# Twelve more u tiles turned during the merge stage, with the loads reordered, out units begun early and the sort spread evenly

## The reference

```
a = att_out @ w_att_branch ; b = ml_out @ w_ml_branch
x = x + (sigmoid(ga) * a + sigmoid(gb) * b) @ w_out
q = norm(x) @ wq ; s = q . sub_keys ; top 16 per half, then top 16 of the sums
out = sum over picks of g * gelu(u[pick] . xn) * v[pick]
```

## Time and profile before

| | |
|---|---|
| median of 3 runs | 1986.28 us (1985.18 to 1992.99) |
| profiled execution | 1996.68 us, span 1994.9 us, mean granted PE clock 0.979 |
| busy shares of the span | PE 96%, VectorE 69%, ACT 44%, POOL 39% |
| project | 0 to 480.5 us |
| merge | 480.5 to 611.5 us |
| queries | 611.5 to 680 us |
| search, steps 0 to 127 | 680 to 1396.2 us |
| experts and finish | 1396.2 to 1994.9 us |

### The profile page before, as it was taken

How to read it: one execution, slowest core, us unless ns; L and a number is a source line. 1 busy time by engine, 2 the same in 40 slices (tenths; PEclk the granted TensorE clock), 3 DMA queues, 4 the chain that set the end, 5 groups by cost and what they waited for, 6 DMA issues and landing times. The chain is left out here.

```text
span 1994.9 us, 32364 instructions
## 1 busy us (share of the span) xinstructions
PE 1907.0 (96%) x11569; PEld 1810.7 (91%) x11569; DVE 1368.2 (69%) x2630; ACT 885.1 (44%) x1929; POOL 775.0 (39%) x639
## 2 busy tenths in 40 slices
PE   6999989998798999999999999999999999999998
PEld 6978868887797999999999999999999999999997
DVE  3133555665514399899999877776678777778775
ACT  4031022224314245678787888782333333333333
POOL 4433323332223346665566666571122222222210
PEclk9989989999998999999999999999999999999999
DMA  7612159887552145799999999999799999999982
GB/s 173 115 50 64 43 164 234 263 271 223 195 107 74 47 152 174 243 272 287 283 296 291 285 311 325 311 314 311 247 345 330 352 342 332 352 334 342 352 300 94
DMA packets 325341, 478.79 MB, mean 240 GB/s; under 512 B 37533, under 2 KB 250013, under 8 KB 321853
## 3 DMA queue, kind: packets, MB, share of 16 engines
q1 hardware_dynamic: 287740, 341.63, 55.7%
q0 software_dynamic: 36864, 134.23, 20.9%
q10 hardware_dynamic: 576, 0.85, 0.1%
HBM read 391.52 MB, written 83.96 MB: 238 GB/s over the span
## 5 line engine op out<-in xcount | busy, mean ns | idle before, releaser
L1468 PE MATMUL ps<-x_high,split_high 128*128 128x416 f32 x1024 | 370.9, 362 | 18.2 <-DVE split_low L1455 16.9
L1468 PE MATMUL ps<-x_high,split_low 128*128 128x416 f32 x1024 | 362.1, 354 | 0.0
L2111 PE MATMUL ps<-hid_high,split_high 128*128 128x416 f32 x1024 | 358.9, 350 | 1.7 <-PEq L1689 1.7
L1468 PE MATMUL ps<-x_low,split_high 128*128 128x416 f32 x1024 | 360.3, 352 | 0.0
L2111 PE MATMUL ps<-hid_low,split_high 128*128 128x416 f32 x1024 | 358.8, 350 | 0.0
L2111 PE MATMUL ps<-hid_high,split_low 128*128 128x416 f32 x1024 | 358.7, 350 | 0.0
L2054 ACT CAST split_high<-area 128x1024 fp32r<-128x1024 f32 x127 | 133.3, 1049 | 383.5 <-PE ps L2111 382.5
L1337 POOL DMA_INDIRECT gathered_rows<-in_peer_v_dram,gathered_index x128 | 133.9, 1046 | 420.0 <-DVE gathered_acc L1374 343.2
L2082 DVE TENSOR_TENSOR split_low<-area,split_high 128x1024 fp32r<-128x1024 f32 x127 | 155.6, 1225 | 134.2 <-ACT split_high L2054 134.2
L1337 POOL DMA_INDIRECT gathered_rows<-in_peer_u_dram,gathered_index x128 | 157.1, 1227 | 215.2 <-DVE gathered_rows L1352 189.3
L1468 PEld LDWEIGHTS ps<-x_high,split_high 128*128 128x128 f32 x1024 | 193.4, 189 | 25.7 <-DVE split_low L1455 21.5
(11 more groups left out here) (299 smaller groups left out, 3844.8 us busy)
## 6 DMA issues: line engine op xcount, KB each, us to landing
area<-in_peer_v_dram SPq DMA_DIRECT2D x128, 512.0 KB, 5.5
u_nat<-in_peer_u_dram SPq DMA_DIRECT2D x392, 128.0 KB, 5.8
routing<-dense SPq DMA_DIRECT2D x26, 1024.0 KB, 6.5
area<-hidden SPq DMA_DIRECT2D x128, 208.0 KB, 7.3
hidden<-gelu_out SPq DMA_DIRECT2D x124, 208.0 KB, 4.7
w_raw<-in_w_in_dram SPq DMA_DIRECT2D x44, 512.0 KB, 5.8
mv_nat<-in_peer_u_dram SPq DMA_DIRECT2D x120, 128.0 KB, 3.6
u_nat<-turned_u SPq DMA_DIRECT2D x30, 512.0 KB, 3.7
```

Source lines behind the costliest of these rows:

```text
L1468: ins = self.nc.tensor.matmul(self.k.ps[:, b, 0:N], w[:, b, kk, :], x[:, kk, 0:N], start=(kk == 0 and p == 0), stop=(kk == KD - 1 and p == 2))
L2111: ins = nc.tensor.matmul(ps[:, kk, 0:N], v[:, b, kk * P:(kk + 1) * P], h[:, b, :], start=(n == 0 and p == 0), stop=(n == P - 1 and p == 2))
```

## The change

Three things are changed. Tiles 30 to 41 are turned ahead too, in the merge, by the same code, which becomes a class `Ahead`: six turns follow the branch units 5, 7, ... 15 on VectorE, six follow the adds of out units 1, 3, ... 11. SP's list in the merge is put in another order: gate blocks 0 and 1 without a wait, chunk 2 before gate blocks 2 and 3, x not before c = 3; tile loads and stores come in from c = 3 on, before the query weights where the list has them so, and the last six tiles' stores and loads after all query weights. The out units take all eight banks, and the first four of them do the first six of their eight blocks of rows as soon as 12 low halves are there and the gated products of unit 13 are done. In the search the plan's credit is 1.5 from step 28 on where it was 1.8 from step 30, so the fourth and fifth frame tiles are sorted at steps 54 and 84. Buffers: the squares of the norm go into the gates' tile, which makes room for the turned tiles.

```
-AHEAD = 30
+EARLIER, MERGED = 30, 12
+AHEAD = EARLIER + MERGED
...
+    BEGUN, FIRST_PART = 4, 6
...
+    BESIDE_BRANCH = MERGED // 2
+    def turned_by(u):
+        return [EARLIER + (u - 5) // 2] if u >= 5 and u % 2 else []
+    def turned_in(u):
+        return [EARLIER + BESIDE_BRANCH + u // 2] if u % 2 and u // 2 < MERGED - BESIDE_BRANCH else []
+    def slot(j):
+        return (j + 2) % RING
...
+            def turned_ones(first, count):
+                for n in range(first, first + count):
+                    ahead.store(sp, n)
+                    if n + 2 < AHEAD:
+                        ahead.load(sp, n + 2)
...
                 if c == 1:
+                    for j in range(2):
+                        load_gates(j)
+                if c == 2:
                     sp.wait_ge(mo_used, 4)
-                    for j in range(RING):
+                    for j in range(2, RING):
                         load_gates(j)
+                if c == 3:
                     sp.dma_start(x[:, 0:4, :], x_prompt[0].rearrange("(t p) d -> p t d", p=P)).then_inc(x_loaded, 16)
...
+                if c == 3:
+                    for n in range(EARLIER, EARLIER + 2):
+                        ahead.load(sp, n)
+                if 4 <= c < 7:
+                    turned_ones(EARLIER + 2 * (c - 4), 2)
                 if c == 6:
...
             load_queries(1)
+            turned_ones(EARLIER + BESIDE_BRANCH, MERGED - BESIDE_BRANCH)
             sp.wait_ge(k.loaded, 16 * QUARTERS)
+            for h in range(2):
+                sp.wait_ge(k.u_stored[h], 16 * AHEAD)
...
-            pe.wait_ge(merged_low_done, 2 * KD - 1)
...
-                if u >= 4:
-                    pe.wait_ge(out_added, u - 3)
-                for kk in range(KD):
+                if u >= 8:
+                    pe.wait_ge(out_added, u - 7)
+                for kk in range(lo, hi):
...
+            pe.wait_ge(merged_low_done, 2 * FIRST_PART)
+            pe.wait_ge(a_used, 2 * (2 * KD - 2))
+            for u in range(BEGUN):
+                out(u, 0, FIRST_PART)
+            pe.wait_ge(merged_low_done, 2 * KD)
+            for u in range(BEGUN):
+                out(u, FIRST_PART, KD)
+            for u in range(BEGUN, OUTS):
+                out(u, 0, KD)
...
                 nc.vector.tensor_tensor(merged_low[:, j, h * HALF:(h + 1) * HALF], merged[:, h, :], merged_high[:, j, h * HALF:(h + 1) * HALF],
                                         ALU.subtract).then_inc(merged_low_done, 1)
+                for n in turned_by(u):
+                    ahead.turn(dve, n)
...
+                for n in turned_in(u):
+                    ahead.turn(dve, n)
...
+class Ahead:
+    def load(self, sp, n):
+        after(sp, self.k.u_turned, n - 1)
+        load_quarters(sp, self.nat[:, n % 2, :], self.peer_u, n, self.k.tile_loaded[3 + n % 2])
+    def turn(self, dve, n):
+        dve.wait_ge(self.k.tile_loaded[3 + n % 2], 16 + 16 * QUARTERS * (n // 2 + 1))
+        after(dve, self.k.u_stored[n % 2], 32 * (n // 2))
...
-                    credit += 4.3 if n < 12 else 4.3 if n < 24 else 2.9 if n < AHEAD else 1.8
+                    credit += 4.3 if n < 24 else 2.9 if n < 28 else 1.5
```

More of the change, by code:

```diff
@@ L408, in turned_at @@
     def turned_at(u):
[L410 to L429, removed]
+        return [n for n in range(EARLIER) if CLEAR + n * (2 * GATE_TILES - CLEAR) // EARLIER == u]
+    ahead = Ahead(nc, k, peer_u, ahead_nat, ahead_turned)
     def wqk_of(q):
@@ L569, in _ @@
         def _(act):
-            norm_scalar(nc, k, act, 0, xn, x_loaded, [16] * NT)
+            norm_scalar(nc, k, act, 0, [xn[:, t, :] for t in range(NT)], x_loaded, [16] * NT)
             act.wait_ge(g1_loaded, 16)
@@ L1034, in _, with merge @@
                     weigh_values(u - 2)
-def merge(nc, k, hold, x_prompt, x_sample, w_att_branch, w_ml_branch, w_out, norm2_g, peer_wq):
+def merge(nc, k, hold, x_prompt, x_sample, w_att_branch, w_ml_branch, w_out, norm2_g, peer_wq, peer_u):
     ps, x, aqT, mqT = k.ps, k.x, k.aqT, k.mqT
@@ L1064, in merge @@
     OUTS = NT * D // W
-    squares = hold("squares", [P, NT, D])
+    BEGUN, FIRST_PART = 4, 6
+    squares = [gate[:, 0:4].rearrange("p a g t -> p (a g t)")[:, t * D:(t + 1) * D] for t in range(4)] + [hold("squares", [P, D])[:, :]]
+    ahead_nat = hold("merge_u_nat", [P, 2, D])
+    ahead_turned = hold("merge_u_turned", [P, 2, 2, D // 2])
+    ahead = Ahead(nc, k, peer_u, ahead_nat, tuple(tuple(ahead_turned[:, n, i, :] for i in range(2)) for n in range(2)))
+    BESIDE_BRANCH = MERGED // 2
[5 more added lines that the diff above has]
+        return (j + 2) % RING
     with nc.Block() as block:
@@ L1218, in _ @@
                 xs = x[0:r, t, i * W:(i + 1) * W]
-                nc.vector.tensor_tensor(xs, ps[0:r, 4 + u % 4, 0:W], xs, ALU.add).then_inc(out_added, 1)
+                nc.vector.tensor_tensor(xs, ps[0:r, u % 8, 0:W], xs, ALU.add).then_inc(out_added, 1)
+                for n in turned_in(u):
+                    ahead.turn(dve, n)
                 if u >= OUTS - NT + 2:
@@ L1230, in load_quarters, with __init__, store @@
                       table[0, n * P:(n + 1) * P, a * D // QUARTERS:(a + 1) * D // QUARTERS].rearrange("(g i) d -> i g d", i=BLK)).then_inc(loaded, 16)
+class Ahead:
+    def __init__(self, nc, k, peer_u, nat, turned):
+        self.nc, self.k, self.peer_u, self.nat, self.turned = nc, k, peer_u, nat, turned
+    def load(self, sp, n):
[4 more added lines that the diff above has]
+        after(dve, self.k.u_stored[n % 2], 32 * (n // 2))
+        for i in range(2):
+            kk = slice(i * KD // 2, (i + 1) * KD // 2)
+            ins = self.nc.vector.transpose(self.turned[n % 2][i].bitcast(U32).rearrange("p (b g i) -> p g b i", b=KD // 2, i=BLK),
+                                           self.nat[:, n % 2, :].bitcast(U32).rearrange("p (g b j) -> p g b j", g=P // BLK, j=BLK)[:, :, kk, :])
+        ins.then_inc(self.k.u_turned, 1)
+    def store(self, sp, n):
+        sp.wait_ge(self.k.u_turned, n + 1)
+        for i in range(2):
+            sp.dma_start(self.k.turned_dram[n, :, i * KD // 2:(i + 1) * KD // 2, :].rearrange("p b i -> p (b i)"), self.turned[n % 2][i]
+                         ).then_inc(self.k.u_stored[n % 2], 16)
 def fold(ap):
@@ L2156, in _ @@
         def _(act):
-            norm_scalar(nc, k, act, 2, y, [added] * NT, [t + 1 for t in range(NT)])
+            norm_scalar(nc, k, act, 2, [y[:, t, :] for t in range(NT)], [added] * NT, [t + 1 for t in range(NT)])
         @block.vector
```

29 lines of the change are left out of this document (12 added, 17 removed).

## The result

The changed kernel took 1982.31 us (median of 15 runs, 1975.34 to 1985.23) where the kernel before took 1993.56 in 15 runs beside it: a ratio of 0.9939 [0.9926, 0.9951], or 12.2 us less by that ratio (the two medians are 11.3 us apart). That is faster by more than 0.5%, as forecast, but the time lies outside the range given, 1964.5 to 1977.0. The profiled execution took 1975.34 us, the quickest of the 15, span 1973.5.

The account below looks back on a forecast made before the run. VectorE was taken to hold PE up in the search, and a ScalarE-VectorE chain in the merge. Search -13.0 and merge -4.8 made -17.8 us: 1968.5 us from the median of 1986.28, range 1964.5 to 1977.0.

Parts of the forecast that it names:

- Search: Products 28 to 84: relieving VectorE, which holds PE up, gains 13.5 us, taken as 13.0, between 8 and 15.
- the step sum of 52.3: Search steps 28 to 39: VectorE's work after the change, 52.3 us by step prices, against PE's 66.1.
- (a): Merge, branches: weight chunk 2 issued ahead of eight gate loads and x ends ScalarE's wait, -3.2 us.
- (d): Merge, first out product: PE waits for unit 13's gated products instead of the fifteenth merged half, -4.2 us.
- (b): Merge, branches: of six turns on VectorE, those after units 5 and 9 cost 0.8 us each, +1.6.
- (c): Merge, branches: turns wait for their tiles and delay VectorE's later work, 0 to 3 us, taken 0.5.
- (e): Merge, out products: six turns hidden, but tile 38's load stands behind query weights; 0 to 3 us, taken 0.5.
- Only the search gains: Rival: the merge's turns wait for their tiles and eat its 4.8 us; -13.0, 1973.3 us, chance 0.18.
- rule of the ring: DMA engines consume a queue's descriptors in ring order, so tile 38 cannot pass the query weights.
- Another engine takes over: Rival: DMA or ScalarE holds the pace in steps 40 to 84; only 9.8 us gained, 1976.5, chance 0.12.
- The turns only change place: Rival: all 12 turns fall on the merge's chain, 16.3 us; -3.1 in all, 1983.2 us, chance 0.07.
- The slower rival: Out products: tile 38 landing after about 585 costs PE each us; gain used up at 603; chance 0.03.

Follow-up runs that it names:

- e1: The kernel before with only the new credit of the sort, 30 tiles turned ahead and the old merge: 1984.26 us, ratio 0.9972.
- e4: The changed kernel without the twelve turned tiles; loads, early out units, eight banks and pace stay: 1975.45 us, ratio 0.9912.
- e7: e6 with a sort credit of 2.4 in steps 24 to 39 and 1.4 from step 40 on: 1973.4 us, ratio 0.99.
- e2: The changed kernel with the old credit of the sort: 1986.52 us, ratio 0.9972.
- e8: e4 with PE starting the out units as the kernel before did, eight banks kept: 1981.6 us, ratio 0.9939.
- e6: e3 with x loaded behind tiles 30 and 31: 1979.75 us, ratio 0.9924.
- e3: The changed kernel with SP issuing the loads of tiles 38 to 41 before both halves of the query weights: 1971.41 us, ratio 0.9893.
- e5: The changed kernel with the query weights issued by ScalarE behind its cast of weight chunk 6, not by SP: 1976.64 us, ratio 0.9908.

## Why the prediction was wrong, and where it was right

**Search: right in size, half right in the reason.** The view by stages and the step prices carried. 71.1 was to become 66.1 and became 66.1; 263.4 was to become 254.9 and became 255.1. For the first number the prediction had VectorE's sum over all of steps 28 to 39 as the limit. The loss sat in products 28 to 32 alone, and with the new pace and no turned tiles (e1, e4) it was above all one tile's late landing that held PE, at one place, and not a sum that presses in every step. For the second VectorE was to lead with 253.4 us against PE's 250.2, but of PE's waits 1.2 us are for its split and 3.4 for POOL and ScalarE, and e7 took 5 us off VectorE for 1.3 of time. That 254.9 was met so closely is in part luck. VectorE was busy 55.6 of 66.0 us in products 28 to 39, 84% where "under 80%" was written, with three pieces of the sort fewer than before: the step sum of 52.3 was 3.3 too low. PE's waits for the split were to fall under 4 and fell to 1.2 us. e1 and e2 show that both parts of the edit were needed, one for each stretch.

**Merge (a) and (d): right.** Taken at 3.2 and 4.2. The order of the loads measured 4.2 (before against e8, which also has the eight banks and the new pace) and the early start 4.1 us (e8 against e4). The 1.0 us by which (a) gave more than ScalarE's wait was not followed up.

**Merge (b) and (c): near, as far as one profile shows.** Between e4 and the changed kernel the branches differ by 3.2 us. Of these tile 30's wait is 2.18, in the bounds of 0 to 3 but above the 0.5 taken; what is left for the turns is 1.0, with 1.6 taken. The same branches with tile loads differ by 2.5 us between e6 and e7, so neither term is measured better than that.

**Merge (e): the step that failed.** The step said that tile 38 lands near 583, that PE asks at about 586.5, cost taken 0.5, bounds 0 and 3. The mechanism was named, with every transfer ahead of tile 38; the term was mis-sized. It measured 5.9 us (64.2 us of out products against 58.3). PE asked where it was to ask: by the changed kernel's clock, 4.9 us earlier, at 581.6, and it was 581.9. The tile was to land at 578.1 by that clock and landed at 584.3. Half of these 6.2 us were lost before the query weights: their first half was to go out at 551.1 and went out at 554.22, behind the load of tile 37 and four small loads (g) that took SP 2.93 us. The other half came behind it: 30.1 us from there to the landing where 27 were taken, from the earlier trace rows, a row of a kernel in which no tile loads or stores shared the queue, and from two terms of 3 us that no row shows. SP's 8.30 us for the second half lie within the 30.1. Then, a wait of 4.16 us on PE brought a stretch at the lower clock, 1.5 us, that no bound contained.

The sum of the merge, -4.2 - 4.1 + 1.0 + 2.2 + 5.9 = +0.8, meets the +1.0 in the table. With the search's -13.2 that makes -12.2 us, as the ratio has it; but the interval of the ratio is 9.8 to 14.8 us and each term comes from single profiles, so the agreement to a tenth is chance. The stages that the prediction left alone differ by a few us either way between executions and are not counted.

**The rivals.** "Only the search gains" is what came, by the mechanism written for it: the tiles' loads behind x and the query weights ate the merge's 4.8 us. It had 0.18. Its rule of the ring was held at 0.5 us of cost; the row of 11.4 us beside it already spoke for more. "Another engine takes over" came in kind, with the 3.4 us for POOL and ScalarE, and not in size: products 40 to 84 still gained 8.2. "The turns only change place" is true of the merge's half in a sense: 9.1 us paid for 5.9. The slower rival had the right place and the right threshold: each us after 585, which is 580.1 on the changed kernel's clock, was to be a us of PE. Tile 38 landed 4.2 us after that, and PE waited 4.16; it would have had to be 18.

**The base and the range.** Two things together put the time outside the range. The sum started from the median of three runs, 1986.28, which is 7.3 us under the 1993.56 of all fifteen, and the range had no room for that, though the three themselves went up to 1992.99. Moved up by 7.3 us the range would have ended at 1984.3, with 1982.31 inside. And without the 5.4 us by which (e) was short, 1976.9 would have been just inside the range as it stood. "Only the search gains" had 1973.3, inside the range, so by its own base the prediction's range allowed for what came.

For the gain the base doesn't count. Against 1993.56 us the predicted 17.8 us would have made 1975.8 for a measured 1982.31; of the miss, 5.6 us by the ratio (0.9910 for 0.9939), 5.4 are (e), and the rest, (c) 1.7 more and (a) and (b) 1.6 less, nearly cancels. With only that step mended, e3 measured 0.9893 [0.9872, 0.9913], an interval which holds the predicted ratio. e3 beats both kernels; e7 (0.99) can't be told from it.

## What to carry to other kernels

When loads are put behind others in one queue, price the wanted one by the moment at which the first of the others can go out and by all the bytes ahead of it, at the pace of a queue that is full, not by a row from a quiet stretch. A load that an engine waits for goes ahead of one that only the next stage needs; eight banks of slack hid some 20 us of lateness here, not 25. A stretch in which an engine is full is worth taking apart product by product: here the loss sat in five of twelve. And a change of several parts is worth undoing one part at a time: this one, at 12 us, held a part, the twelve turns in their first order, that by itself lost more than it gave.

## What the runs showed of the hardware that was not expected

The issue of four transfers of 512 KB cost SP 1.93 us for the first half of the query weights and 8.30 us for the second, which followed it by 3.4 us with weight chunk 7 between. In the kernel before, with 12.2 us from one half to the other, both were short:

```profile
547.34 1.93 SPq L1076 DMA_DIRECT2D area<-in_peer_wq_dram  x4
...
559.53 2.09 SPq L1076 DMA_DIRECT2D area<-in_peer_wq_dram  x4
```

ScalarE, issuing all eight in e5, was held for 10.13 us. And a wait of 4.16 us on PE was followed by 3.5 us at the lower granted clock, one of 2.39 us in e1 by some 3 us of slow matmuls, while the out products of e3, without such a wait, kept 1.00 in 585 to 590 us:

```profile
585.00:590.00 5.00, 5.00 (x45) 4.88 (x44) 0.84 (x2) 0.00 (x0) 0.00 (x0) 1.00 1.08 209
```
